# First two weight pieces of an input projection in one pass over x, loaded by the scalar engine's queue

## Chip, cores and metric

One core of a Trainium2 chip. The metric is the device time of one execution in microseconds, median over runs.

## What is computed

One layer of an encoder: neighbourhood attention beside a gated short convolution, a cross attention to a memory, and an expert-choice mixture of 16 SwiGLU experts, each followed by a layer norm. The change is in the very first product, `x @ w_in`. Cut to what matters:

```python
D_MODEL, SEQ = 1024, 512           # x: (1, 512, 1024) float32, w_in: (1024, 3072)
def hybrid_mixer(x, w_in, rpb, conv_w, w_out):
    proj = x @ w_in
    q, k, v, b_gate, c_gate, h = jnp.split(proj, [512, 1024, 1536, 2048, 2560], axis=-1)
    y_na = neighbourhood_attention(heads(q), heads(k), heads(v), rpb)
    y_conv = b_gate * short_conv(c_gate * h, conv_w)
    return jnp.concatenate([y_na, y_conv], axis=-1) @ w_out
x = layer_norm(DN_ALPHA * x + hybrid_mixer(...), ...)
x = layer_norm(DN_ALPHA * x + memory_cross_attention(...), ...)
x = layer_norm(DN_ALPHA * x + expert_choice_moe(...), ...)
```

## The kernel before

The dense weights lie in HBM as chunks of 128 partitions x 4096 floats. Chunks 0 to 7 are worked off in pieces of 1024 columns, 32 pieces in all. A piece is 8 blocks (`KT`) of 128x128: for each of the 8 blocks of x's 1024 channels, the weights of 128 output channels. Piece 0 to 3 are chunk 0, the query weights. x comes turned: block k is `x_raw[:, k, :]`, 128 channels x 512 tokens.

The products are made in parts. ScalarE rounds the weights and x to a shorter float (`hi`: `first_hi`/`hi_split` for weights, `x_hi` for x). What is left over is subtracted out: on GpSimd for the weights (`lo`, `first_lo`/`lo_split`), on VectorE for x (`x_lo`). A piece then takes 24 products of TensorE, 128x128 by 128x512, summed in one bank: 8 of hi with x_hi (L829), 8 of hi with x_lo (L831), 8 of lo with x_hi (L834). There is room for two pieces in parts (`piece[:, p % 2]`), so piece p's rounding waits until piece p - 2 has been used (`piece_used`). Banks `pj[0]` and `pj[1]` take turns in the same way (`proj_kept`), and ScalarE copies each finished bank out.

The order of the work is written out by hand, one list for each engine:

- The sync engine (SP) issues x's first transfer (blocks 0 and 1), piece 0, x's other three transfers, pieces 1 to 3, then chunk 1 and chunk 2 whole, the memory, constants and the bias (L436 to L447), and from there on waits for pieces before it loads the next chunk. All these go by one queue.
- ScalarE, L618 to L625: x block 0, half of piece 0 (4 blocks), x blocks 1 to 3, the other half of piece 0, x blocks 4 to 7, piece 1, and the tokens at the grid's edge (`edge_x`). Then for each piece its rounding and the copy of an older bank.
- GpSimd, L526 to L541: the low parts of piece 0 in two halves, then piece by piece.
- VectorE: `kv` is set to ones, then `x_lo` of the 8 blocks (L1393), then the edge's (L1396).
- TensorE: two filler products of ones whose result is not used (L887), then piece 0 in the order in which x's blocks come (`first_from_x`, L873 to L882), then pieces 1 to 7 (`from_x`), the value pieces, and so on.

Much later the 403 MB of expert weights flow through the same sync queue into an eight-slot ring; each of their loads waits for a count of TensorE's progress (`projected`, `scored`, `exp_used`).

Of the kernel before, what the change touches and what calls it, by code (L numbers as in the profile page):

```python
# [6 lines left out]
F32 = mybir.dt.float32  # L7
# [5 lines left out]
P = 128  # L13
# [90 lines left out]
PIECES = 32  # L104
# [20 lines left out]

START_FILLERS = 2


def build(nc, x, x_turned, mem_turned, dense, na_bias, conv_w, ln1_g, ln1_b,
          ln2_g, ln2_b, router, experts, ln3_g, ln3_b, consts, out):  # L130
    with ExitStack() as ctx:
# [3 lines left out]
        def sem(name):  # L135
            return ctx.enter_context(nc.semaphore(name))
# [128 lines left out]
        x_in = [sem(f"x_in{m}") for m in range(KT // 2)]  # L265
        first_in = sem("first_in")
        first_hi, first_lo, ones_set = sem("first_hi"), sem("first_lo"), sem("ones_set")
        res_in = sem("res_in")
        q_in = [sem(f"q_in{m}") for m in range(1, 4)]
        mem_in, cst_in, small_in = (sem(n) for n in ("mem_in", "cst_in", "small_in"))  # L270
# [48 lines left out]
        def pre_flat(c):  # L319
            return ring[:, PRE_SLOT[c] * SLOT:(PRE_SLOT[c] + 1) * SLOT]  # L320
# [12 lines left out]
        def raw_piece(p):  # L333
            flat = pre_flat(PIECE_CHUNK[p])[:, 1024 * (p % 4):1024 * (p % 4) + 1024]
            return flat.rearrange("p (k n) -> p k n", k=KT)

        def piece_used(eng, p):
# [67 lines left out]
        def _(sp):  # L405
# [19 lines left out]
            def load_x(m):  # L425
                k = slice(2 * m, 2 * m + 2)
                sp.dma_start(x_raw[:, k, :], x_turned[:, k, :]).then_inc(x_in[m], 16)

            def load_first():
                sp.dma_start(raw_piece(0), dense[0, :, 0:1024].rearrange("p (k n) -> p k n", k=KT)).then_inc(first_in, 16)  # L430

            def load_q(m):
                sp.dma_start(raw_piece(m), dense[0, :, 1024 * m:1024 * m + 1024].rearrange("p (k n) -> p k n", k=KT))\
                    .then_inc(q_in[m - 1], 16)

            load_x(0)  # L436
            load_first()
            for m in range(1, KT // 2):
                load_x(m)
            for m in range(1, 4):  # L440
                load_q(m)
# [5 lines left out]
            sp.dma_start(bias_room[1], na_bias[:, 4096:6144]).then_inc(bias_in, 16)  # L447
            sp.wait_ge(lo_split, 3)
            load_pre(CH_MK)
            sp.wait_ge(lo_split, 7)  # L450
            load_pre(CH_MV)
            sp.wait_ge(lo_split, 11)
            load_pre(5)
            for c, done in ((6, 15), (7, 19), (CH_OUT, 23), (CH_OUT + 1, 27)):
                sp.wait_ge(lo_split, done)
                load_pre(c)
# [67 lines left out]
        def _(pool):  # L524
            nc.gpsimd.memset(neg_half, -0.5).then_inc(half_set, 1)
            for a in range(2):  # L526
                k = slice(4 * a, 4 * a + 4)
                pool.wait_ge(first_hi, a + 1)
                nc.gpsimd.tensor_tensor(piece[:, 0, 1, k, :], raw_piece(0)[:, k, :], piece[:, 0, 0, k, :].bitcast(F32),
                                        ALU.subtract).then_inc(first_lo, 1)  # L530
# [7 lines left out]

            for p in range(1, PIECES):
                pool.wait_ge(hi_split, p)  # L540
                nc.gpsimd.tensor_tensor(piece[:, p % 2, 1, :, :], raw_piece(p), piece[:, p % 2, 0, :, :].bitcast(F32),  # L541
                                        ALU.subtract).then_inc(lo_split, 1)
                if p in POOL_EARLY:
                    out_low(POOL_EARLY[p])
# [34 lines left out]
        def _(act):  # L579
# [10 lines left out]
            def split(p):  # L590
                if p < 4:
                    act.wait_ge(q_in[p - 1], 16)
                else:
                    chunk_in(act, PIECE_CHUNK[p])
                if p >= 2:
                    piece_used(act, p - 2)
                nc.scalar.activation(piece[:, p % 2, 0, :, :], raw_piece(p), ACT.Copy).then_inc(hi_split, 1)  # L597
# [13 lines left out]

            def split_first(a):
                k = slice(4 * a, 4 * a + 4)
                act.wait_ge(first_in, 16)
                nc.scalar.activation(piece[:, 0, 0, k, :], raw_piece(0)[:, k, :], ACT.Copy).then_inc(first_hi, 1)

            split_x(0)
            split_first(0)  # L618
            for k in range(1, 4):
                split_x(k)  # L620
            split_first(1)
            for k in range(4, KT):
                split_x(k)
            split(1)
            nc.scalar.activation(edge_x[0].rearrange("p k (s t) -> p k s t", s=2), edge_tokens(x_raw), ACT.Copy)                .then_inc(edge_hi_kept, 1)  # L625
# [30 lines left out]
            for u in range(NU):  # L656
# [10 lines left out]
                if u == NU - 1:  # L667
                    act.wait_ge(lo_split, PIECES - 1)
                    chunk_in(act, CH_OUT + 1)
                    split_out(4)  # L670
                    act.wait_ge(pv_done, u - 1)
                    keep_turn(TN_NA + u, prT[u % 2])
# [15 lines left out]
                if u == 7:  # L688
                    chunk_in(act, CH_OUT)
                    split_out(0)  # L690
                elif u == 12:
                    act.wait_ge(lo_split, PIECES - 3)
                    split_out(1)
                elif u == 14:
                    act.wait_ge(projected, PIECE_PJ[PIECES - 2] + 1)
                    split_out(2)
# [115 lines left out]
        def _(pe):  # L812
# [8 lines left out]
            def from_x(p):  # L821

                n = PIECE_PJ[p]
                hi, lo = piece[:, p % 2, 0], piece[:, p % 2, 1]
                if n >= 2:
                    pe.wait_ge(proj_kept[n % 2], n // 2)
                pe.wait_ge(hi_split, p)
                for k in range(KT):
                    nc.tensor.matmul(pj[n % 2][:, :], hi[:, k, :], x_hi[:, k, :], start=k == 0, stop=False)  # L829
                for k in range(KT):  # L830
                    nc.tensor.matmul(pj[n % 2][:, :], hi[:, k, :], x_lo[:, k, :], start=False, stop=False)  # L831
                pe.wait_ge(lo_split, p)
                for k in range(KT):
                    mm = nc.tensor.matmul(pj[n % 2][:, :], lo[:, k, :], x_hi[:, k, :], start=False, stop=k == KT - 1)  # L834
                mm.then_inc(projected, 1)
# [10 lines left out]
            def v_from_x(p):  # L846
# [4 lines left out]
                if k0 == 0:  # L851
                    pe.wait_ge(edge_hi_kept, 1)
                    pe.wait_ge(edge_lo_kept, 1)
                pe.wait_ge(hi_split, p)
                for j in range(2):
                    for a in range(4):
                        nc.tensor.matmul(px[a][:, :], key_x(0, k0 + j, a), hi[:, j, :], start=k0 + j == 0, stop=False)
                        nc.tensor.matmul(px[a][:, :], key_x(1, k0 + j, a), hi[:, j, :], start=False, stop=False)
                pe.wait_ge(lo_split, p)
                for j in range(2):  # L860
# [5 lines left out]
            def first_from_x():  # L866

                hi, lo = piece[:, 0, 0], piece[:, 0, 1]
                for k in range(KT):
                    if k % 4 == 0:  # L870
                        pe.wait_ge(first_hi, k // 4 + 1)
                    pe.wait_ge(x_hi_kept, k + 1)
                    nc.tensor.matmul(pj[0][:, :], hi[:, k, :], x_hi[:, k, :], start=k == 0, stop=False)  # L873
                    if k:
                        pe.wait_ge(x_lo_kept, k)
                        nc.tensor.matmul(pj[0][:, :], hi[:, k - 1, :], x_lo[:, k - 1, :], start=False, stop=False)
                pe.wait_ge(x_lo_kept, KT)
                nc.tensor.matmul(pj[0][:, :], hi[:, KT - 1, :], x_lo[:, KT - 1, :], start=False, stop=False)
                for k in range(KT):
                    if k % 4 == 0:  # L880
                        pe.wait_ge(first_lo, k // 4 + 1)
                    mm = nc.tensor.matmul(pj[0][:, :], lo[:, k, :], x_hi[:, k, :], start=False, stop=k == KT - 1)  # L882
                mm.then_inc(projected, 1)
# [4 lines left out]
            first_from_x()  # L888
            for p in range(1, 8):
                from_x(p)  # L890
# [9 lines left out]
            def mem_k(p):  # L900
# [3 lines left out]
                pe.wait_ge(mem_lo_split, 2)  # L904
                pe.wait_ge(hi_split, p)
# [4 lines left out]
                pe.wait_ge(lo_split, p)  # L910
                for k in range(KT):
# [3 lines left out]
            def mem_v(p):  # L915
# [8 lines left out]
                pe.wait_ge(hi_split, p)  # L924
# [5 lines left out]
                pe.wait_ge(lo_split, p)  # L930
                last = p == MV_PIECES[-1]
# [924 lines left out]
```

## Time and profile before

| what | value |
|---|---|
| median of 3 runs | 1253.47 us (1252.36 to 1255.1) |
| profiled execution | known by its span, 1250.1 us from the first to the last instruction; no own time is listed for it |
| median less that span | 3.4 us |
| TensorE busy | 1167.7 us, 93% of the span |
| DMA | 444.65 MB, mean 356 GB/s |

A busy TensorE isn't one that sets the time: its rows overlap its waits, and the DMA engines are nearly full from about 310 us to the end. The chain of work that ended last tells which of the two held the end at each moment. Times in the views are microseconds from the first instruction. SPq and ACTq are the queues of DMA issues of the sync and the scalar engine; in the DMA views they are q1 and q10. The share in a DMA queue's row is that of 16 engines' time in the stretch.

### The profile page before, as it was taken

What the parts mean: (1) busy time and instruction counts of PE and PEld (TensorE: products, weight loads), DVE (VectorE), ACT (ScalarE), POOL (GpSimd) and SP (SyncE); (2) the same over time, 40 slices, a digit from 0 to 9 for tenths busy, and PEclk for the clock granted to TensorE, in tenths of its full rate; (3) what the DMA queues carried; (4) which work ended last, traced back from release to release, by engine and by line L of the source; (5) the groups of instructions that cost most, each with busy time, mean ns of one, the idle gap of its engine ahead of it and who ended that gap; (6) DMA issues with size and microseconds to landing.
All of it is one profiled execution on the core that took longest, in us unless ns stands there. A gap on an engine that the chain in (4) does not pass through costs nothing.

```text
span 1250.1 us, 13617 instructions
## 1 busy us (share of the span) xinstructions
PE 1167.7 (93%) x5780; PEld 588.4 (47%) x5780; DVE 258.4 (21%) x485; ACT 194.3 (16%) x355; POOL 137.9 (11%) x69
## 2 busy tenths in 40 slices
PE   8999999999999999998899889988997998899996
PEld 6887778888733433432243324323432432243332
DVE  3032557627600010010001000200110020002013
ACT  4244444142000000010000001000000000000021
POOL 4454334331002000000000000000000000000001
PEclk9999999999999999999999999999999999999999
DMA  9432222247799999999999999999999999999996
GB/s 374 177 135 80 92 96 105 115 186 329 299 380 428 431 412 430 426 435 434 431 427 434 433 431 430 434 432 428 434 431 432 429 434 432 430 427 428 427 428 254
DMA packets 28068, 444.65 MB, mean 356 GB/s; under 512 B 4480, under 2 KB 4864, under 8 KB 9728
## 3 DMA queue, kind: packets, MB, share of 16 engines
q1 hardware_dynamic: 25728, 441.89, 83.9%
q10 hardware_dynamic: 2304, 2.24, 0.5%
q8 instruction: 27, 0.44, 0.1%
q14 instruction: 9, 0.07, 0.0%
HBM read 442.02 MB, written 2.10 MB: 355 GB/s over the span
## 4 chain that ended last, share of the span: by engine, by line
PE 65%; DMA 30%; DVE 2%; ACT 1%; issue 1%; POOL 0%; SPq 0%; DVEq 0%; POOLq 0%; ACTq 0%
DMA ring<-in_w_exp 30%; PE bank L1317 17%; PE bank L1365 14%; PE bank L1188 5%; PE bank L1279 4%; PE bank L829 3%; PE bank L831 3%; PE bank L834 3%; PE bank L1013 1%; PE bank L1015 1%; PE bank L1014 1%; PE bank L1247 1%; PE bank L818 1%; PE bank L1349 1%; PE bank L969 1%
## 5 line engine op out<-in xcount | busy, mean ns | idle before, releaser
L1317 PE MATMUL bank<-ring,yt 128*64 128x512 f32 x2000 | 450.3, 604 | 43.5 <-DMA ring<-in_w_exp 43.4
L1317 PEld LDWEIGHTS bank<-ring,yt 128*64 128x64 f32 x2000 | 145.4, 139 | 337.1 <-issue 287.7
L1365 PE MATMUL bank<-ring,yt 128*64 128x512 f32 x944 | 214.2, 607 | 21.5 <-DMA ring<-in_w_exp 16.6
L1365 PEld LDWEIGHTS bank<-ring,yt 128*64 128x64 f32 x944 | 68.0, 139 | 146.8 <-issue 130.3
L1717 DVE TENSOR_TENSOR work<-bank,work 128x512 f32<-128x512 f32 x32 | 22.1, 692 | 378.0 <-PE bank L1317 378.0
L767 ACT ACTIVATE work<-bank 128x512 f32<-128x512 f32 x32 | 19.1, 597 | 484.5 <-PE bank L1317 484.5
L552 POOL TENSOR_SCALAR stat<-stat 128x1 f32<-128x1 f32 x4 | 2.5, 618 | 832.5 <-ACT work L808 832.4
L541 POOL TENSOR_TENSOR piece<-ring,piece 128x1024 fp32r<-128x1024 f32 x31 | 74.3, 2397 | 91.2 <-ACT piece L597 91.2
L1728 DVE TENSOR_TENSOR xT<-bank,xT 128x512 f32<-128x512 f32 x56 | 38.7, 692 | 137.1 <-PE bank L1279 137.1
L1188 PE MATMUL bank<-yt,res 128*128 128x128 f32 x512 | 60.0, 276 | 0.0
L1188 PEld LDWEIGHTS bank<-yt,res 128*128 128x128 f32 x512 | 58.4, 192 | 0.8 <-issue 0.8
L1279 PE MATMUL bank<-yt 128*128 128x512 f32 x112 | 54.5, 619 | 0.0
L771 ACT ACTIVATE yt<-bank 128x512 f32<-128x512 f32 x31 | 18.5, 597 | 198.5 <-PE bank L1349 194.5
L597 ACT ACTIVATE piece<-ring 128x1024 fp32r<-128x1024 f32 x31 | 32.8, 1059 | 89.8 <-PE bank L834 56.8
L829 PE MATMUL bank<-x_hi,piece 128*128 128x512 f32 x152 | 39.3, 401 | 0.0
L831 PE MATMUL bank<-x_lo,piece 128*128 128x512 f32 x152 | 37.6, 390 | 0.0
L834 PE MATMUL bank<-x_hi,piece 128*128 128x512 f32 x152 | 37.6, 390 | 0.0
L784 ACT ACTIVATE yt<-bank 64x512 f32<-64x512 f32 x28 | 16.5, 591 | 129.8 <-PE bank L1365 129.4
L1279 PEld LDWEIGHTS bank<-yt 128*128 128x128 f32 x112 | 17.8, 188 | 36.4 <-DVE xT L1728 18.4
L1679 DVE COPY yt<-bank 128x512 f32<-128x512 f32 x16 | 11.1, 692 | 106.9 <-PE bank L1188 106.9
L1709 DVE COPY yt<-bank 128x512 f32<-128x512 f32 x7 | 4.8, 692 | 131.2 <-PE bank L1295 131.2
L829 PEld LDWEIGHTS bank<-x_hi,piece 128*128 128x128 f32 x152 | 27.6, 188 | 8.2 <-issue 2.0
(246 smaller groups left out, 1072.7 us busy)
## 6 DMA issues: line engine op xcount, KB each, us to landing
ring<-in_w_exp SPq DMA_DIRECT2D x66, 4096.0 KB, 29.9
ring<-in_w_exp SPq DMA_DIRECT2D x39, 2048.0 KB, 29.1
ring<-in_dense SPq DMA_DIRECT2D x12, 2048.0 KB, 7.8
ring<-in_w_exp SPq DMA_DIRECT2D x6, 3072.0 KB, 28.3
ring<-in_w_exp SPq DMA_DIRECT2D x14, 1024.0 KB, 28.0
ring<-in_x_turned SPq DMA_DIRECT2D x4, 512.0 KB, 6.6
ring<-in_dense SPq DMA_DIRECT2D x4, 512.0 KB, 9.2
res<-in_na_bias SPq DMA_DIRECT2D x1, 2048.0 KB, 27.1
```

The costliest lines, as they stand in the source:

```text
L541: nc.gpsimd.tensor_tensor(piece[:, p % 2, 1, :, :], raw_piece(p), piece[:, p % 2, 0, :, :].bitcast(F32), ALU.subtract).then_inc(lo_split, 1)
L597: nc.scalar.activation(piece[:, p % 2, 0, :, :], raw_piece(p), ACT.Copy).then_inc(hi_split, 1)
L767: nc.scalar.activation(silu[g], bank[2 * g][:, :], ACT.Silu).then_inc(silu_done, 1)
L829: nc.tensor.matmul(pj[n % 2][:, :], hi[:, k, :], x_hi[:, k, :], start=k == 0, stop=False)
L831: nc.tensor.matmul(pj[n % 2][:, :], hi[:, k, :], x_lo[:, k, :], start=False, stop=False)
L834: mm = nc.tensor.matmul(pj[n % 2][:, :], lo[:, k, :], x_hi[:, k, :], start=False, stop=k == KT - 1)
L1188: mm = nc.tensor.matmul(pv[k // 4][:, P * (k % 4):P * (k % 4) + P], res[:, t, P * k:P * k + P], pick[:, t].rearrange("p e n -> p (e n)"), ...
L1279: mm = nc.tensor.matmul(pv[(c + 1) % 2][:, :], scat[:, t, :], ye[:, 512 * n:512 * n + 512], start=True, stop=True)
L1317: mm = nc.tensor.matmul(bank[2 * g + n % 2][64 * c:64 * c + 64, :], xeT[:, kk, 64 * e:64 * e + 64], exp_rhs(j, first, k, c), start=kk == 0 ...
L1365: mm = nc.tensor.matmul(bank[5][64 * n:64 * n + 64, :], hidT[:, s, 64 * c:64 * c + 64], exp_rhs(j, first, s, n), start=(g, c, s) == (0, 0, ...
L1717: nc.vector.tensor_tensor(hid[g], bank[2 * g + 1][:, :], silu[g], ALU.mult).then_inc(hid_ready, 1)
L1728: nc.vector.tensor_tensor(y, pv[(c + 1) % 2][:, :], y, ALU.add).then_inc(mix_kept, 1)
```

## The change

Pieces 0 and 1 are taken together in one pass over x's blocks. They are loaded as four transfers (`FIRST_LOADS`), each with two blocks of both pieces, by ScalarE's queue ahead of its first rounding. In HBM each partition's part of such a transfer is two runs of 256 floats. The sync queue no longer loads pieces 0 and 1. ScalarE rounds a transfer's 128 x 512 elements between the two x blocks of the same number, GpSimd makes low parts by transfer. TensorE does both pieces' products block by block; the low products of piece 0 are mixed in, those of piece 1 follow at the end. There are three start fillers for two, and a half-wide one inside each of the first three blocks. The counts of `hi_split` and `lo_split` now start at piece 2, which `nth(p)` takes care of wherever they are waited for.

```diff
-START_FILLERS = 2
+START_FILLERS = 3
+FIRST_PIECES = 2
+FIRST_LOADS = KT // 2
...
-        first_in = sem("first_in")
+        first_in = [sem(f"first_in{g}") for g in range(FIRST_LOADS)]
...
+        def nth(p):
+            return p - FIRST_PIECES + 1
+
+        def first_raw(g):
+            flat = pre_flat(0)[:, 0:1024 * FIRST_PIECES]
+            return flat.rearrange("p (a k n) -> p a k n", a=FIRST_PIECES, k=KT)[:, :, 2 * g:2 * g + 2, :]
+
+        def first_part(g, part):
+            return piece[:, :, part, 2 * g:2 * g + 2, :]
...
-            load_x(0)
-            load_first()
-            for m in range(1, KT // 2):
+            for m in range(KT // 2):
                 load_x(m)
-            for m in range(1, 4):
+            for m in range(FIRST_PIECES, 4):
                 load_q(m)
...
-            for a in range(2):
-                k = slice(4 * a, 4 * a + 4)
-                pool.wait_ge(first_hi, a + 1)
-                nc.gpsimd.tensor_tensor(piece[:, 0, 1, k, :], raw_piece(0)[:, k, :], piece[:, 0, 0, k, :].bitcast(F32),
+            for g in range(FIRST_LOADS):
+                pool.wait_ge(first_hi, g + 1)
+                nc.gpsimd.tensor_tensor(first_part(g, 1), first_raw(g), first_part(g, 0).bitcast(F32),
                                         ALU.subtract).then_inc(first_lo, 1)
...
-            def split_first(a):
-                k = slice(4 * a, 4 * a + 4)
-                act.wait_ge(first_in, 16)
-                nc.scalar.activation(piece[:, 0, 0, k, :], raw_piece(0)[:, k, :], ACT.Copy).then_inc(first_hi, 1)
-
-            split_x(0)
-            split_first(0)
-            for k in range(1, 4):
-                split_x(k)
-            split_first(1)
-            for k in range(4, KT):
-                split_x(k)
-            split(1)
+            def load_first(g):
+                src = dense[0, :, 0:1024 * FIRST_PIECES].rearrange("p (a k n) -> p a k n", a=FIRST_PIECES, k=KT)
+                act.dma_start(first_raw(g), src[:, :, 2 * g:2 * g + 2, :]).then_inc(first_in[g], 16)
+
+            def split_first(g):
+                act.wait_ge(first_in[g], 16)
+                nc.scalar.activation(first_part(g, 0), first_raw(g), ACT.Copy).then_inc(first_hi, 1)
+
+            for g in range(FIRST_LOADS):
+                load_first(g)
+            for g in range(FIRST_LOADS):
+                split_x(2 * g)
+                split_first(g)
+                split_x(2 * g + 1)
...
             def first_from_x():
 
-                hi, lo = piece[:, 0, 0], piece[:, 0, 1]
+                def product(n, k, w, of, stop=False):
+                    return nc.tensor.matmul(pj[n][:, :], piece[:, n, w, k, :], of[:, k, :],
+                                            start=k == 0 and w == 0 and of is x_hi, stop=stop)
+
                 for k in range(KT):
-                    if k % 4 == 0:
-                        pe.wait_ge(first_hi, k // 4 + 1)
+                    if k % 2 == 0:
+                        pe.wait_ge(first_hi, k // 2 + 1)
                     pe.wait_ge(x_hi_kept, k + 1)
-                    nc.tensor.matmul(pj[0][:, :], hi[:, k, :], x_hi[:, k, :], start=k == 0, stop=False)
+                    for n in range(FIRST_PIECES):
+                        product(n, k, 0, x_hi)
+                    if k < 3:
+                        nc.tensor.matmul(px[0][:, 0:256], kv[:, 0:P], kv[:, 0:256], start=True, stop=True)
                     if k:
                         pe.wait_ge(x_lo_kept, k)
-                        nc.tensor.matmul(pj[0][:, :], hi[:, k - 1, :], x_lo[:, k - 1, :], start=False, stop=False)
+                        for n in range(FIRST_PIECES):
+                            product(n, k - 1, 0, x_lo)
+                    if k % 2 and k > 1:
+                        pe.wait_ge(first_lo, k // 2)
+                        for m in (k - 3, k - 2):
+                            product(0, m, 1, x_hi)
                 pe.wait_ge(x_lo_kept, KT)
-                nc.tensor.matmul(pj[0][:, :], hi[:, KT - 1, :], x_lo[:, KT - 1, :], start=False, stop=False)
-                for k in range(KT):
-                    if k % 4 == 0:
-                        pe.wait_ge(first_lo, k // 4 + 1)
-                    mm = nc.tensor.matmul(pj[0][:, :], lo[:, k, :], x_hi[:, k, :], start=False, stop=k == KT - 1)
+                product(0, KT - 1, 0, x_lo)
+                pe.wait_ge(first_lo, FIRST_LOADS)
+                for m in (KT - 2, KT - 1):
+                    mm = product(0, m, 1, x_hi, stop=m == KT - 1)
+                mm.then_inc(projected, 1)
+                product(1, KT - 1, 0, x_lo)
+                for m in range(KT):
+                    mm = product(1, m, 1, x_hi, stop=m == KT - 1)
                 mm.then_inc(projected, 1)
...
-            for p in range(1, 8):
+            for p in range(FIRST_PIECES, 8):
                 from_x(p)
```

ScalarE at the start of the program, before (line numbers of the kernel before; `ring` holds the raw weights and x):

```order
L610 ACT_TABLE_LOAD
L610 ACTIVATE x_hi<-ring 128x512 [waits x_in0]
L615 ACTIVATE piece<-ring 128x512 [waits first_in]
L610 ACTIVATE x_hi<-ring 128x512 [waits x_in0]
L610 ACTIVATE x_hi<-ring 128x512 [waits x_in1] x2
L615 ACTIVATE piece<-ring 128x512 [waits first_in]
L610 ACTIVATE x_hi<-ring 128x512 [waits x_in2] x2
L610 ACTIVATE x_hi<-ring 128x512 [waits x_in3] x2
L597 ACTIVATE piece<-ring 128x1024 [waits q_in1]
```

And with the change (line numbers of the changed kernel):

```order
L619 DMA ring<-in_dense 128x2x256 x4
L615 ACT_TABLE_LOAD
L615 ACTIVATE x_hi<-ring 128x512 [waits x_in0]
L623 ACTIVATE piece<-ring 128x2x256 [waits first_in0]
L615 ACTIVATE x_hi<-ring 128x512 [waits x_in0]
...
L615 ACTIVATE x_hi<-ring 128x512 [waits x_in3]
L623 ACTIVATE piece<-ring 128x2x256 [waits first_in3]
L615 ACTIVATE x_hi<-ring 128x512 [waits x_in3]
L631 ACTIVATE edge_x_70<-ring 128x1024
L602 ACTIVATE piece<-ring 128x1024 [waits projected,q_in2]
```

Four DMA issues stand ahead of the table load, and the rounding of x's last block now follows a wait for the fourth weight transfer.

TensorE at x's blocks 6 and 7, before:

```order
L873 MATMUL bank<-x_hi,piece 128x512 [waits x_hi_kept]
L876 MATMUL bank<-x_lo,piece 128x512 [waits x_lo_kept]
L878 MATMUL bank<-x_lo,piece 128x512 [waits x_lo_kept]
L882 MATMUL bank<-x_hi,piece 128x512 [waits first_lo]
L882 MATMUL bank<-x_hi,piece 128x512 x3
L829 MATMUL bank<-x_hi,piece 128x512 [waits hi_split]
```

And with the change, from block 6 to the first product of piece 2:

```order
L875 MATMUL bank<-x_hi,piece 128x512 [waits x_hi_kept,first_hi]
L875 MATMUL bank<-x_hi,piece 128x512
L875 MATMUL bank<-x_lo,piece 128x512 [waits x_lo_kept]
...
L875 MATMUL bank<-x_hi,piece 128x512 [waits x_hi_kept]
...
L875 MATMUL bank<-x_hi,piece 128x512 [waits first_lo]
...
L875 MATMUL bank<-x_lo,piece 128x512
L875 MATMUL bank<-x_hi,piece 128x512 x8
L835 MATMUL bank<-x_hi,piece 128x512 [waits hi_split,proj_kept0]
```

Block 6's products now wait for a weight transfer of their own (`first_hi`), where only x was waited for; the next piece is piece 2 and waits for bank 0's copy too.

## Rows read from the trace of the kernel before

**Rows 1.** The page: span, and the chain's shares by line

```profile
span 1250.1 us, 13617 instructions
...
DMA ring<-in_w_exp 30%; PE bank L1317 17%; PE bank L1365 14%; PE bank L1188 5%; PE bank L1279 4%; PE bank L829 3%; PE bank L831 3%; PE bank L834 3%; PE bank L1013 1%; PE bank L1015 1%; PE bank L1014 1%; PE bank L1247 1%; PE bank L818 1%; PE bank L1349 1%; PE bank L969 1%
```

**Rows 2.** Chain of waits, 0 to 22 us: start us, us, what

```profile
1.65 6.16 DMA ring<-in_x_turned
...
10.06 3.45 DVE x_lo L1393 x4
...
19.52 1.81 PE bank L834 x8
```

**Rows 3.** Chain of waits, whole span: the first long wait for a DMA

```profile
489.72 22.18 DMA ring<-in_w_exp
```

**Rows 4.** Three issuing lines: duration ns, first and last start us; time to landing

```profile
L427 SPq DMA_DIRECT2D ring<-in_x_turned x4: 384/428/840, 0.7 to 2.6; - x4
...
DMA to landing us min/median/max: 4.0/6.6/7.8
...
L433 SPq DMA_DIRECT2D ring<-in_dense x3: 446/447/466, 3.5 to 4.5; - x3
...
DMA to landing us min/median/max: 8.8/9.6/10.4
...
L407 SPq DMA_DIRECT2D ring<-in_dense x2: 440/470/500, 5.0 to 5.5; - x2
...
DMA to landing us min/median/max: 14.8/16.9/19.1
```

**Rows 5.** DMA queues, 0 to 60 us: packets, MB, share of 16 engines

```profile
q1 hardware_dynamic: 2304, 17.02, 72.0%
q10 hardware_dynamic: 1728, 0.15, 2.6%
```

**Rows 6.** DMA queues, 40 to 41 us

```profile
DMA packets 79, 0.05 MB, mean 55 GB/s; under 512 B 43, under 2 KB 78, under 8 KB 78
...
q10 hardware_dynamic: 78, 0.04, 19.9%
```

**Rows 7.** DMA queues at 275 to 276 us, then at 36 to 37 us

```profile
q1 hardware_dynamic: 22, 0.36, 87.3%
q10 hardware_dynamic: 20, 0.08, 20.5%
...
q1 hardware_dynamic: 26, 0.41, 96.8%
q10 hardware_dynamic: 27, 0.00, 1.5%
```

**Rows 8.** Timeline of the start, and one stretch with clock (ninth column) by windows

```profile
1.45 3.70 PE L887 MATMUL bank<-kv 128*128 128x512 f32 x4 [1.45 <-DVE kv L1390]
...
4.78 0.63 ACT L610 ACTIVATE x_hi<-ring 128x512 fp32r<-128x512 f32 x1 [2.76 <-DMA ring<-in_x_turned]
...
6.25 0.63 ACT L615 ACTIVATE piece<-ring 128x512 fp32r<-128x512 f32 x1 [0.84 <-DMA ring<-in_dense]
...
6.93 1.02 PE L873 MATMUL bank<-x_hi,piece 128*128 128x512 f32 x2 [1.78 <-ACT piece L615]
...
10.39 0.63 PE L873 MATMUL bank<-x_hi,piece 128*128 128x512 f32 x1
...
10.82 0.63 PE L876 MATMUL bank<-x_lo,piece 128*128 128x512 f32 x1
...
12.30 1.06 ACT L597 ACTIVATE piece<-ring 128x1024 fp32r<-128x1024 f32 x1 [0.72 <-DMA ring<-in_dense]
...
8.30:11.70 3.40, 3.18 (x7) 2.13 (x7) 3.34 (x5) 3.29 (x7) 1.55 (x1) 0.51 1.02 365
```

**Rows 9.** ScalarE's DMA issues: one line's durations, and one long issue

```profile
L587 ACTq DMA_DIRECT2D cw<-in_conv_w x3: 448/521/528, 32.4 to 33.4; - x3
...
33.94 4.60 ACTq L588 DMA_DIRECT2D wr<-in_router  x1
```

More of the change, by code:

```diff
@@ L265, in build @@
         x_in = [sem(f"x_in{m}") for m in range(KT // 2)]
-        first_in = sem("first_in")
+        first_in = [sem(f"first_in{g}") for g in range(FIRST_LOADS)]
         first_hi, first_lo, ones_set = sem("first_hi"), sem("first_lo"), sem("ones_set")
         res_in = sem("res_in")
-        q_in = [sem(f"q_in{m}") for m in range(1, 4)]
+        q_in = [sem(f"q_in{m}") for m in range(FIRST_PIECES, 4)]
         mem_in, cst_in, small_in = (sem(n) for n in ("mem_in", "cst_in", "small_in"))
@@ L427, in load_x @@
                 sp.dma_start(x_raw[:, k, :], x_turned[:, k, :]).then_inc(x_in[m], 16)
-            def load_first():
-                sp.dma_start(raw_piece(0), dense[0, :, 0:1024].rearrange("p (k n) -> p k n", k=KT)).then_inc(first_in, 16)
             def load_q(m):
                 sp.dma_start(raw_piece(m), dense[0, :, 1024 * m:1024 * m + 1024].rearrange("p (k n) -> p k n", k=KT))\
-                    .then_inc(q_in[m - 1], 16)
-            load_x(0)
-            load_first()
-            for m in range(1, KT // 2):
+                    .then_inc(q_in[m - FIRST_PIECES], 16)
+            for m in range(KT // 2):
                 load_x(m)
-            for m in range(1, 4):
+            for m in range(FIRST_PIECES, 4):
                 load_q(m)
@@ L447, in _ @@
             sp.dma_start(bias_room[1], na_bias[:, 4096:6144]).then_inc(bias_in, 16)
-            sp.wait_ge(lo_split, 3)
+            sp.wait_ge(lo_split, nth(3))
             load_pre(CH_MK)
-            sp.wait_ge(lo_split, 7)
+            sp.wait_ge(lo_split, nth(7))
             load_pre(CH_MV)
-            sp.wait_ge(lo_split, 11)
+            sp.wait_ge(lo_split, nth(11))
             load_pre(5)
             for c, done in ((6, 15), (7, 19), (CH_OUT, 23), (CH_OUT + 1, 27)):
-                sp.wait_ge(lo_split, done)
+                sp.wait_ge(lo_split, nth(done))
                 load_pre(c)
@@ L537, in out_low @@
                 nc.gpsimd.tensor_tensor(lo, raw, hi.bitcast(F32), ALU.subtract).then_inc(out_lo_pool, 1)
-            for p in range(1, PIECES):
-                pool.wait_ge(hi_split, p)
+            for p in range(FIRST_PIECES, PIECES):
+                pool.wait_ge(hi_split, nth(p))
                 nc.gpsimd.tensor_tensor(piece[:, p % 2, 1, :, :], raw_piece(p), piece[:, p % 2, 0, :, :].bitcast(F32),
@@ L591, in split @@
                 if p < 4:
-                    act.wait_ge(q_in[p - 1], 16)
+                    act.wait_ge(q_in[p - FIRST_PIECES], 16)
                 else:
                     chunk_in(act, PIECE_CHUNK[p])
-                if p >= 2:
-                    piece_used(act, p - 2)
+                piece_used(act, p - 2)
                 nc.scalar.activation(piece[:, p % 2, 0, :, :], raw_piece(p), ACT.Copy).then_inc(hi_split, 1)
@@ L667, in _ @@
                 if u == NU - 1:
-                    act.wait_ge(lo_split, PIECES - 1)
+                    act.wait_ge(lo_split, nth(PIECES - 1))
                     chunk_in(act, CH_OUT + 1)
@@ L691, in _ @@
                 elif u == 12:
-                    act.wait_ge(lo_split, PIECES - 3)
+                    act.wait_ge(lo_split, nth(PIECES - 3))
                     split_out(1)
@@ L826, in from_x @@
                     pe.wait_ge(proj_kept[n % 2], n // 2)
-                pe.wait_ge(hi_split, p)
+                pe.wait_ge(hi_split, nth(p))
                 for k in range(KT):
@@ L831, in from_x @@
                     nc.tensor.matmul(pj[n % 2][:, :], hi[:, k, :], x_lo[:, k, :], start=False, stop=False)
-                pe.wait_ge(lo_split, p)
+                pe.wait_ge(lo_split, nth(p))
                 for k in range(KT):
@@ L853, in v_from_x @@
                     pe.wait_ge(edge_lo_kept, 1)
-                pe.wait_ge(hi_split, p)
+                pe.wait_ge(hi_split, nth(p))
                 for j in range(2):
@@ L858, in v_from_x @@
                         nc.tensor.matmul(px[a][:, :], key_x(1, k0 + j, a), hi[:, j, :], start=False, stop=False)
-                pe.wait_ge(lo_split, p)
+                pe.wait_ge(lo_split, nth(p))
                 for j in range(2):
@@ L904, in mem_k @@
                 pe.wait_ge(mem_lo_split, 2)
-                pe.wait_ge(hi_split, p)
+                pe.wait_ge(hi_split, nth(p))
                 for k in range(KT):
@@ L909, in mem_k @@
                     nc.tensor.matmul(acc, hi[:, k, :], m_lo[:, k, :], start=False, stop=False)
-                pe.wait_ge(lo_split, p)
+                pe.wait_ge(lo_split, nth(p))
                 for k in range(KT):
@@ L923, in mem_v @@
                         pe.wait_ge(proj_kept[(PJ_MV + t) % 2], (PJ_MV + t) // 2)
-                pe.wait_ge(hi_split, p)
+                pe.wait_ge(hi_split, nth(p))
                 for j in range(2):
@@ L929, in mem_v @@
                                              start=k0 + j == 0 and m is m_hi, stop=False)
-                pe.wait_ge(lo_split, p)
+                pe.wait_ge(lo_split, nth(p))
                 last = p == MV_PIECES[-1]
```

## The prediction

> **What bounds the kernel now.** I read the page first: its chain of waits is TensorE's own lines and, for 30%, transfers of expert weights [rows 1]. In order of time the two parts are apart: from 14 us on the chain is TensorE work and the short steps between its stages, and the first long wait for expert weights comes at 489.72 us [rows 3]. The loads of expert weights are started by TensorE's progress (the waits on projected, scored and exp_used), so a microsecond gained or lost before 14 us moves all behind it by a microsecond, as far as these rows tell. I count it in full.
>
> The chain of the first 22 us [rows 2] tells what sets the start: x's second transfer lands at 7.81, then come ScalarE's roundings of x, then four of VectorE's subtractions (10.06 to 13.51), then the low products of piece 0 and piece 1's 24 products, the last eight from 19.52 to 21.33. From there TensorE goes on without a gap. So 21.33 us, the end of piece 1, is the mark that the change has to beat.
>
> **What the transfers give.** Now x's four transfers, pieces 0, 1, 2, 3 and chunk 1, 2 stand in one queue. x's first is issued at 0.73 and lands 4.0 us later, at 4.8; piece 3, issued at 4.5, lands after 10.4, at 14.9 [rows 4]. In between lie seven transfers of 4 KB rows. Packets are the contiguous runs: in the first 60 us the sync queue moved 2304, which is 16 transfers x 128 rows plus 16 small ones for each transfer, and the scalar queue 1728, which is three conv_w loads of 512 four-byte runs, 128 router rows, and 4 x 16 small ones [rows 5]. Hence on each of 16 DMA engines a load of 128 rows is 8 packets and a small one. The price of a 4 KB packet is (14.9 - 4.8) / 56 = 0.18 us. Chunk 2 (16 KB rows, 16 packets behind piece 3) lands at 5.5 + 19.1 = 24.6: (24.6 - 14.9) / 16 = 0.61 us each. A line through both gives 0.07 us for 1 KB. Its lower bound is a quarter of a 4 KB packet, 0.045, its upper bound a whole one, 0.18. The nearest row: at 40 to 41 us the scalar queue, almost alone, moved 78 packets in 19.9% of 16 engine-microseconds, 43 of them under 512 B, so 35 of about 1 KB at no more than 3.2 / 35 = 0.09 [rows 6]. I take 0.07.
>
> **The change part by part.**
> *Transfers.* Pieces 0 and 1 come as four transfers of 128 x 2 runs of 1 KB: 17 packets on each engine per transfer, 68 in all. They leave on the scalar queue, beside the sync queue's 9 per transfer (x four times, pieces 2 and 3, chunks 1 and 2). What decides is how an engine shares itself between two queues. The trace has it twice: at 275 us both queues are full, the sync queue with 16 KB and the scalar queue with 4 KB packets, and they move 22 against 20; at 36 us it is 26 packets of 16 KB against 27 of 4 bytes [rows 7]. One packet of one, one packet of the other, whatever their size. By this the queue with the many small packets is served last.
>
> Under that alternation a landing is 3.3 us (4.8 less 8 x 0.18) plus everything moved until then. Transfer 0 ends at packet 17: 3.3 + 16 x 0.18 + 16 x 0.07 = 7.3. Transfer 1 at packet 34: 3.3 + 31 x 0.18 + 32 x 0.07 = 11.1. x's fourth at 36: about 11.4. Transfer 2 at 51, of which the other queue has spent 45 on x and pieces 2 and 3: 3.3 + 45 x 0.18 + 48 x 0.07 = 14.8. The sync queue's small loads end at packet 54, so the last 14 packets of transfer 3 each go after one of chunk 1's or 2's, 13 of these with data: 3.3 + 48 x 0.18 + 13 x 0.61 + 64 x 0.07 = 24.4 us. Before, all of pieces 0 and 1 was there at 12.3 [rows 8].
>
> By the Trainium skill ("DMA: Bandwidth & Descriptors", Queues, rings and completion order) an engine drains a whole packet of some 9 to 17 descriptors from one ring before it goes to the next; if a packet there were one transfer's share, the two queues would change over per transfer. The counts of the rows above speak against that reading; it is the first rival below.
>
> *TensorE.* Its order asks for first_hi 4 before the two products of block 6. Of 48 products 26 stand ahead of that (12 with x_hi, 10 with x_lo, 4 low ones), which are through by about 17 us; 22 are left. ScalarE needs 0.63 for the rounding, and TensorE's first product of piece 0 came 0.7 us after its landing (6.25 to 6.93) [rows 8]; so TensorE resumes at 25.1. 22 products at 1.81 / 8 = 0.227 us are 5.0 us. Before them it has been idle some 8 us. The trace shows what that costs: idle from 5.15 to 6.93, it then had a granted clock of 0.51 from 8.3 to 11.7, the 1.2 GHz level, with products 0.43 us apart (10.39, 10.82). Over 3.4 us that is 8 products where 15 were possible, 1.6 us lost. I put in the same once: bounds are 0 and all 22 products, 4.4. End of piece 1: 25.1 + 5.0 + 1.6 = 31.7, against 21.33: +10.4 us.
>
> *ScalarE.* Four DMA issues of about 0.5 us [rows 9] stand before the table load, 2.1 us. It had been idle for 2.76 us before x's first block [rows 8], which now comes later. Cost 0. A long issue like the 4.60 us one, with 1,584 packets queued ahead [rows 9], would add 4.1, 1.3 beyond that idle time, and be hidden as well: until transfer 0 lands at 7.3 one rounding waits. In the new order each block pair's rounding stands behind a wait for its transfer, so x_hi 7, the edge rounding and VectorE's work on both are queued behind transfer 3; all of these are 0.5 to 1 us and end before their products are due (x_hi 7 at 25.6).
> *Fillers.* Two start fillers are four rows in 3.70 us [rows 8], so the third ends at 7.0, and the three small ones inside the pass are half as wide, 0.9 each at most. Products of piece 0 can't start before 8.0 and then wait for every transfer, so they cost 0; if transfers were prompt, they would cost up to 2.8.
> *GpSimd* makes the same low parts in four steps; the last one's first product is due after 11 others, 2.5 to 4.7 us behind the rounding. 0.
> *Sync queue.* Two issues fewer. Chunks 1 and 2 land up to 4.5 us later (64 x 0.07), at 24 and 29; their first users are pieces 4 and 8, whose turns come ten later as well. 0.
>
> **Sum:** +10.4 us on a span of 1250.1, so 1260.5. The runs shown have their median 3.4 us above the span: **1263.9 us**. Case alone: -1.6 for the clock and -1.8 for packets by bytes, +3 for a longer slow clock or dearer packets: 1260.5 to 1267.
>
> **The rivals.**
> *Queues change over per transfer* (the page's reading): transfer 3 lands right behind x's fourth, 3.3 + 32 x 0.18 + 64 x 0.07 = 13.5; resume at 14.2, 22 products, 19.2: 2.1 us ahead, less up to 1.6 if the clock falls as now. 1251.4 to 1253.0, no change that can be told. For it: the rows counted were not at the program's start, when both queues are empty. Against: the same counts with three mixes of size. 0.17.
> *Faster:* the same, and 1 KB packets go by bytes, 0.045: landing at 3.3 + 5.8 + 2.9 = 12.0, and with a full clock, which the fillers hold, TensorE ends at 12.7 + 5.0 = 17.7, 3.6 ahead: 1249.9. The point from which it decides: transfer 3 must land before 13. Against it the 0.09 bound of [rows 6], and 48 products from 7 us on need 10.9 us by themselves. 0.10.
> *Slower still:* a 1 KB packet takes a 4 KB packet's time between two queues, 64 x 0.11 = +7: 1271. 0.05.
> *The transfers aren't split as written* (a row's two runs as one packet of 2 KB): 36 packets in place of 68 would end with x's fourth, the first rival's time; the 1728 packets counted for runs of 4 bytes leave it little; it is within that 0.17.
>
> **How the numbers follow.** Alternation 0.68, slower still 0.05, per transfer 0.17, faster 0.10. A measurement can tell about 0.2%, 2.5 us. Faster 0.10, same 0.17, slower 0.73. The forecast is the likeliest case's 1263.9, its own range 1260.5 to 1267; the range that leaves out no more than 2 in 10 has to take in the per-transfer case: 1251 to 1267.
>
> **What would show it.** In the changed trace: both queues with near equal packet counts from 3 to 15 us; the four dense transfers landing at about 7, 11, 15 and 24 us; TensorE idle from about 17 to 25 for ScalarE's rounding, and ScalarE for a DMA into ring; a granted clock of 0.5 behind it; the first product of piece 2 at 31 to 32. If the fourth lands by 14, the alternation is wrong at the start of a program and so is the forecast; if it lands at 24 and the time rises by less than 7, the loss does not carry to the end.

## The result and the profile after

The changed kernel takes 1260.38 us (median of 4 runs, 1259.24 to 1262.87), the kernel before 1253.36 us beside it. The ratio is 1.0060, 95% interval 1.0048 to 1.0072: slower by 6.0 to 9.0 us. The forecast was 1263.9 us, range 1251 to 1267; the time also lies just under the likeliest case's own range, 1260.5 to 1267.

The chain of waits of the changed kernel, 0 to 40 us (start us, us, what), answers to [rows 2]:

```profile
2.29 18.97 DMA ring<-in_dense
...
21.27 0.64 ACT piece L623
...
21.96 7.89 PE bank L875 x22
29.84 1.81 PE bank L835 x8
```

The chain's first DMA wait is no longer for x but for the fourth weight transfer, issued at 2.29 and landed at 21.25 us. Piece 1 ends at 29.84 us, where it ended at 21.33: 8.5 us later. Its landings by issuing line, which answer to [rows 4]:

```profile
L619 ACTq DMA_DIRECT2D ring<-in_dense x4: 482/486/1073, 0.7 to 2.3; - x4
...
DMA to landing us min/median/max: 5.1/10.0/19.0
```

The DMA queues of the changed kernel at 4, 7, 9, 14 and 16 us, one microsecond each (packets, MB, share of 16 engines; q1 the sync queue, q10 ScalarE's):

```profile
q10 hardware_dynamic: 143, 0.15, 49.1%
q1 hardware_dynamic: 41, 0.10, 36.7%
...
q1 hardware_dynamic: 82, 0.33, 80.5%
q10 hardware_dynamic: 82, 0.08, 23.6%
...
q1 hardware_dynamic: 83, 0.32, 79.6%
q10 hardware_dynamic: 83, 0.08, 22.8%
...
q1 hardware_dynamic: 27, 0.44, 104.2%
q10 hardware_dynamic: 28, 0.03, 8.2%
...
q1 hardware_dynamic: 27, 0.44, 104.5%
q10 hardware_dynamic: 26, 0.03, 7.7%
```

From 7 to 18 us the counts are nearly equal in each microsecond (58 against 53 where they differ most), whatever the sizes: 82 against 82 and 83 against 83 with x's 4 KB packets, 27 against 28 and 27 against 26 with the 16 KB packets of chunks 1 and 2. Before 7 us they are not: at 4 to 5 us ScalarE's queue moved 143 packets and the sync queue 41, and when the first weight transfer was through, at 5.9 us, 272 against 210. What shares the engines out there is not shown. From 14 us on the weights that TensorE waits for get 0.03 MB in a microsecond, and chunks 1 and 2, whose first user is piece 4 with its first product at 40.7 us, get 0.44.

What ScalarE and TensorE do meanwhile, in the timeline (start us, us, engine, line, op; behind it the idle time before and what ended it):

```profile
9.99 0.63 ACT L623 ACTIVATE piece<-ring 128x512 fp32r<-128x512 f32 x1 [1.93 <-DMA ring<-in_dense]
...
13.15 0.63 ACT L623 ACTIVATE piece<-ring 128x512 fp32r<-128x512 f32 x1 [1.49 <-DMA ring<-in_dense]
...
15.78 0.61 PE L875 MATMUL bank<-x_hi,piece 128*128 128x512 f32 x2
21.27 0.63 ACT L623 ACTIVATE piece<-ring 128x512 fp32r<-128x512 f32 x1 [6.45 <-DMA ring<-in_dense]
...
21.96 1.22 PE L875 MATMUL bank<-x_hi,piece 128*128 128x512 f32 x2 [5.56 <-ACT piece L623]
```

And by windows (busy us and count of PE, PEld, DVE, ACT, POOL, then the granted clock, the DMA share, GB/s):

```profile
16.00:21.90 5.90, 0.40 (x2) 0.00 (x0) 0.30 (x1) 0.63 (x2) 0.00 (x0) 0.90 1.04 438
21.90:27.30 5.40, 5.34 (x13) 4.18 (x14) 2.49 (x2) 1.47 (x3) 1.28 (x1) 0.50 1.02 425
```

TensorE is idle for 5.6 us, and behind that its granted clock is 0.50, the 1.2 GHz level, for 5.4 us: 12 or 13 products where 24 would fit. The shift is carried along: a row of the chain that stood at 455.42 us before stands at 464.04, 8.6 later (before, then with the change).

```profile
455.42 17.32 PE bank L1317 x80
...
464.04 17.32 PE bank L1337 x80
```

### The profile page after: what moved, and what is told of

The parts are those of the page before. It is cut to its first block, busy times and chain, and to the rows that moved or that the text cites. A ratio compares the mean times of both kernels' runs of the same rounds, so it can differ in the third digit from the quotient of the medians.

```text
span 1261.0 us, 13639 instructions
## 1 busy us (share of the span) xinstructions
PE 1172.9 (93%) x5788; PEld 591.7 (47%) x5788; DVE 258.0 (20%) x485; ACT 194.7 (15%) x356; POOL 137.8 (11%) x70
## 4 chain that ended last, share of the span: by engine, by line
PE 64%; DMA 31%; DVE 2%; ACT 1%; issue 1%; POOL 0%; ACTq 0%; DVEq 0%; SPq 0%; POOLq 0%
DMA ring<-in_w_exp 30%; PE bank L1337 17%; PE bank L1385 14%; PE bank L1208 5%; PE bank L1299 4%; PE bank L835 3%; PE bank L837 3%; PE bank L840 3%; DMA ring<-in_dense 2%; PE bank L1033 1%; PE bank L1035 1%; PE bank L1034 1%; PE bank L1267 1%; PE bank L824 1%; PE bank L1369 1%; PE bank L989 1%
## 5 line engine op out<-in xcount | busy, mean ns | idle before, releaser
L835 PE MATMUL bank<-x_hi,piece 128*128 128x512 f32 x144 | 37.3, 401 | 0.0
L840 PE MATMUL bank<-x_hi,piece 128*128 128x512 f32 x144 | 35.6, 389 | 0.0
L1699 DVE COPY yt<-bank 128x512 f32<-128x512 f32 x16 | 11.1, 692 | 106.9 <-PE bank L1208 106.9
```

## The experiments

All are edits of the changed kernel. The last column is the median and the ratio to the kernel before with its interval; "end of piece 1" is the chain's row of the first product of piece 2.

| kernel | fourth transfer landed | end of piece 1 | chain's mark near 455 us | median us, ratio |
|---|---|---|---|---|
| before | (12.3, piece 1) | 21.33 | 455.42 | 1253.36 |
| changed | 21.25 | 29.84 | 464.04 | 1260.38, 1.0060 (1.0048 to 1.0072) |
| e1 one queue | 12.8 | 19.72 | 453.87 | 1251.16, 0.9987 (0.9978 to 0.9996) |
| e2 sync queue holds back | 11.9 | 20.92 | 455.21 | 1252.09, 0.9998 (0.9989 to 1.0007) |
| e3 runs of 2 KB | 12.8 | 19.99 | 454.16 | 1251.74, 0.9990 (0.9981 to 0.9999) |
| e4 the same, old fillers | 12.3 | 19.93 | 454.08 | 1251.10, 0.9987 (0.9978 to 0.9996) |
| e5 runs of 512 B | 35.5 (third 32.50) | 43.56 | 477.68 | 1275.30, 1.0181 (1.0166 to 1.0197) |
| e6 2 KB in one queue | 12.9 | 19.44 | 455.18 | 1251.06, 0.9987 (0.9978 to 0.9996) |
| e7 chunks held back | 14.6 | 21.42 | 457.10 | 1253.53, 1.0005 (0.9996 to 1.0014) |
| e8 fillers in the idle stretch | 20.9 | 26.85 | 461.07 | 1260.05, 1.0063 (1.0047 to 1.0078) |
| e9 changed once more | 21.5 | 29.68 | 463.84 | 1260.64, 1.0061 (1.0047 to 1.0074) |
| e10 as e8, once more | 21.31 | 27.30 | 461.55 | 1258.56, 1.0045 (1.0032 to 1.0059) |

(e1 to e4 ran beside 1253.50 us of before, e5 to e8 beside 1252.57, e9 and e10 beside 1253.55.)

**e1, one queue.**

```diff
+            def load_first(g):
+                src = dense[0, :, 0:1024 * FIRST_PIECES].rearrange("p (a k n) -> p a k n", a=FIRST_PIECES, k=KT)
+                sp.dma_start(first_raw(g), src[:, :, 2 * g:2 * g + 2, :]).then_inc(first_in[g], 16)
+
             for m in range(KT // 2):
                 load_x(m)
+                load_first(m)
...
-            for g in range(FIRST_LOADS):
-                load_first(g)
```

> The changed kernel with its four weight transfers (still 1 KB runs) issued by the sync engine, each behind the x transfer of its number, nothing on the scalar queue at the start. Theory (an engine alternates packet by packet between two queues, so the queue with many small packets ends behind chunks 1 and 2): in one queue the fourth weight transfer lands when x and itself are through, 12 to 15 us instead of 21.3, and piece 1 ends at 18.8 to 20.6: 0.7 to 2.5 us ahead of the kernel before, so 1250.9 to 1252.7. Rival (runs of 1 KB are slow by themselves, whatever the queue): the fourth lands near 21 and the time stays near 1260.

Its chain, 0 to 32 us:

```profile
2.15 6.58 DMA ring<-in_dense
...
8.75 0.64 ACT piece L628
...
10.60 9.11 PE bank L878 x40
19.72 1.84 PE bank L838 x8
```

The same 1 KB runs, the same order on TensorE: piece 1 ends at 19.72, 1.6 us ahead of the kernel before and 10.1 ahead of the changed one. Behind the small filler of block 2 the chain is 40 products without a wait, so from there TensorE is the bound of the pass. Small runs are not slow by themselves, and the pass and its fillers aren't what cost the time. The time is 0.9987 of before, inside what was expected.

**e2, the sync queue holds back.**

```diff
+            sp.wait_ge(first_in[FIRST_LOADS - 1], 16)
             for m in range(FIRST_PIECES, 4):
                 load_q(m)
```

> The changed kernel, weights still on the scalar queue in 1 KB runs, but the sync engine waits for the fourth of them before it issues piece 2 and all that follows. Alternation theory: only x's 36 packets compete with the 68, the rest go alone; the fourth lands at 12.5 to 13.5, piece 1 ends at about 19, time about 1251, though piece 2 and 3 then land at 16 to 18. Rival (small runs slow): no nearer than 18 us and 1257 or more. Rival (scalar queue served late whatever the other holds): unchanged, 1260.

At 8 to 9 us, with x in the sync queue, and at 10 to 11 us, with nothing more in it:

```profile
q1 hardware_dynamic: 93, 0.32, 79.5%
q10 hardware_dynamic: 93, 0.09, 25.1%
...
q10 hardware_dynamic: 368, 0.36, 108.3%
q1 hardware_dynamic: 5, 0.00, 0.3%
```

ScalarE's queue is untouched, and all that changed is what stands in the other one. As soon as that is empty the weights' rate goes from 93 packets in a microsecond to 368. The fourth transfer landed at 11.9, ahead of the 12.5 to 13.5 expected, but piece 1 ended at 20.92 and not at about 19, since the second transfer is held up by x as it was (9.95 us) and block 2 starts at 10.65. Time as before, 0.9998, 1 us over what was expected.

**e3, runs of 2 KB.** The first 2048 columns of chunk 0 are laid out by transfer, in HBM and on chip:

```diff
+    first = out[0, :, 0:1024 * FIRST_PIECES].reshape(P, FIRST_PIECES, FIRST_LOADS, 2, P)
+    out[0, :, 0:1024 * FIRST_PIECES] = first.transpose(0, 2, 1, 3, 4).reshape(P, -1)
...
-                act.dma_start(first_raw(g), src[:, :, 2 * g:2 * g + 2, :]).then_inc(first_in[g], 16)
+                act.dma_start(pre_flat(0)[:, 512 * g:512 * g + 512], dense[0, :, 512 * g:512 * g + 512])\
+                    .then_inc(first_in[g], 16)
```

> The changed kernel with the first two pieces laid out in HBM and on chip so that each partition's part of a transfer is one run of 2 KB: 9 packets per engine and transfer as x has, same bytes, same two queues. Alternation theory: the fourth weight transfer lands with x's fourth, at 11 to 12.5; TensorE's own work from 6.6 on (48 products and three small fillers, some 12.3 us) then sets the end of piece 1 at about 18.9: 2.4 ahead of before, 1251. If the order of TensorE or the fillers were what costs time, it would stay near 1260.

At 9 to 10 us:

```profile
q1 hardware_dynamic: 78, 0.27, 67.2%
q10 hardware_dynamic: 78, 0.13, 34.6%
```

Two queues again, equal counts again, but now the weights get twice the bytes for each turn, and x a little less. The fourth lands at 12.8, 0.4 behind x's fourth (11 to 12.5 was expected). Piece 1 ends at 19.99, 9.85 us ahead of the changed kernel but 1.1 later than expected, 1251.74 us.

**e4, the old fillers with e3's transfers.**

```diff
-START_FILLERS = 3
+START_FILLERS = 2
...
-                    if k < 3:
-                        nc.tensor.matmul(px[0][:, 0:256], kv[:, 0:P], kv[:, 0:256], start=True, stop=True)
```

> As the 2 KB runs, with two start fillers and none inside the pass, as before the change. If the fillers only cost TensorE time once transfers are prompt, piece 1 ends 1.3 us earlier than with them (about 17.6, 1249.7). If without them the granted clock falls to half for 3.4 us as in the kernel before, it ends 1.6 us later less the 1.3: about the same as with them, 1251 to 1251.5.

TensorE in e4's timeline:

```profile
8.91 1.05 PE L875 MATMUL bank<-x_lo,piece 128*128 128x512 f32 x2
9.77 1.05 PE L875 MATMUL bank<-x_hi,piece 128*128 128x512 f32 x2
...
11.13 0.62 PE L875 MATMUL bank<-x_hi,piece 128*128 128x512 f32 x2
```

From 7.0 to 10.6 us the products are 0.43 us apart (two from 8.91 to 9.77), though the granted clock reads 1.00 there; from 11.1 on 0.23. In e3 the first pair, ahead of any small filler, takes 0.57 us, as a pair behind a wait does later on (9.73 to 10.30); in the changed kernel the first pair takes 0.77, and from the second on all is at full speed. So the third start filler does its work, and the four fillers cost about what the slow products would: 19.93 against 19.99, and no difference in time. That was the second of the two cases expected.

**e5, twice the packets.** Each transfer in two, of one block of both pieces:

```diff
+                for k in range(2):
+                    act.dma_start(first_raw(g)[:, :, k:k + 1, :], src[:, :, 2 * g + k:2 * g + k + 1, :])\
+                        .then_inc(first_in[g], 16)
```

> The changed kernel with each weight transfer cut into two of 512 B runs: the same bytes on the same queue in twice the packets, 136 on each engine instead of 68. Alternation theory: the sync queue has given 54 packets when x and pieces 2 and 3 are through (13 to 14 us); then the scalar queue's other 82 each wait for one of chunks 1 and 2 and of the loads behind them (54 packets, to about 36 us), so the fourth pair lands at 30 to 36 and the time is 1270 to 1277. Rival (a packet costs a fixed time of its own, at most 0.1 us): 64 packets more are at most 6 us more, the fourth at 25 to 27 and the time near 1266 at most.

The DMA queues at 20 to 21 us, and the chain:

```profile
q1 hardware_dynamic: 27, 0.44, 104.2%
q10 hardware_dynamic: 26, 0.01, 4.3%
```

```profile
3.75 28.75 DMA ring<-in_dense
...
33.21 10.36 PE bank L877 x32
43.56 1.84 PE bank L837 x8
```

The weights' bytes fall to 0.01 MB in a microsecond. The chain's row ends with the third pair, at 32.50 us, where the third transfer landed at 13.1 in the changed kernel; TensorE's 32 products stand behind it. The last pair landed at 35.5, 14.3 later than the fourth transfer of the changed kernel, for 64 packets with data more on each engine: 0.22 us each, more than any packet of 512 B takes by itself (e2 moved 1 KB packets at 16 / 368 = 0.043 us). The time, 1275.3 us, is what the alternation gave; the rival's bound was 1266.

**e7, only chunks 1 and 2 held back.**

```diff
+            sp.wait_ge(first_in[FIRST_LOADS - 1], 16)
             load_pre(1)
```

> The changed kernel with chunks 1 and 2 alone held back until the fourth weight transfer has landed; pieces 2 and 3 still go beside it. Alternation theory: the loss comes from the 16 KB packets, so the fourth lands at 14.5 to 15 instead of 21.3, TensorE is idle for under 1 us, piece 1 ends at 20 to 21, time 1252 to 1253.5. If pieces 2 and 3 were the load that pushed it back, it would stay above 1257.

```profile
1.77 11.35 DMA ring<-in_dense
...
13.83 7.59 PE bank L876 x32
21.42 1.84 PE bank L836 x8
```

The chain now passes through the third transfer (issued 1.77, landed 13.12); the fourth is no longer in it. Piece 1 ends 8.4 us earlier than in the changed kernel and 0.1 later than before; the time is that of before. So the 8.5 us lie in the 16 KB packets of chunks 1 and 2. Pieces 2 and 3 beside the weights cost 0.5 (e2, without them, ended at 20.92). That it ended at 21.42 and not by 21, as expected, comes with the third transfer, which landed at 13.12, no earlier than in the changed kernel.

**e8, e9 and e10, the clock.** Six filler products where TensorE is idle:

```diff
                 for k in range(KT):
+                    if k == 6:
+                        for _ in range(6):
+                            nc.tensor.matmul(px[0][:, :], kv[:, 0:P], kv[:, 0:512], start=True, stop=True)
```

> The changed kernel with six full-width filler products put before block 6, in TensorE's idle time (16 to 21.9 us); the transfers are untouched. After the fourth transfer the 22 products took 7.9 us, where 22 x 0.227 are 5.0. Theory (the half clock behind the idle stretch costs the 2.9): the granted clock stays 1.0, piece 1 ends at 27 instead of 29.8 and the time is 1257 to 1258. Rival (the products wait for VectorE and GpSimd anyway): 29 or more and 1260.

In e8 the products behind the fourth transfer (chain, then the window in which the changed kernel had a clock of 0.50; L881 is the six fillers, two rows each):

```profile
16.47 5.15 PE bank L881 x12
21.62 5.23 PE bank L875 x22
26.85 1.84 PE bank L835 x8
```

```profile
21.90:27.30 5.40, 5.40 (x25) 4.45 (x24) 2.50 (x2) 2.98 (x5) 2.24 (x2) 1.00 1.01 419
```

With the clock kept, the 22 products take 5.2 us, not 7.9. But the time came out at 1260.05 us, ratio 1.0063 (1.0047 to 1.0078), where 1257 to 1258 was expected. Since e8 and the changed kernel had been compared across chips and with four runs each, both went again, on one chip.

> The changed kernel once more, beside the next one on the same chip, since the earlier comparison of the two was across chips and with four runs each. Start shift 8.6 us; if it carries in full the ratio is 1.0069, near 1261 to 1262 against 1253.

> The changed kernel with six filler products in the idle stretch, once more, same chip as the changed kernel. Its profile had piece 1 done 3.0 us earlier and the shift unchanged at 461 us, but its time was no lower. Theory (all behind the start carries, the earlier runs differ by the spread of the expert stream): 2.5 to 3.5 us under the changed kernel, ratio to before 1.0045. Rival (the expert stream gives back what is gained): within 1 us of the changed kernel.

The chains of e9 and of e10 behind the fourth transfer:

```profile
22.21 7.47 PE bank L875 x22
```

```profile
22.02 5.29 PE bank L875 x22
```

The changed kernel took 1260.64 us (ratio 1.0061, 1.0047 to 1.0074), about 1 us under what was expected, the one with fillers 1258.56 (1.0045, 1.0032 to 1.0059): 2.1 us less, between the 2.5 to 3.5 of the theory and the rival's 1. In these two profiles the mark near 455 us stands at 463.84 and 461.55, 2.3 apart. On this chip what the clock cost carried to the end: each of the five runs with fillers was faster than each of the five without, 1259.51 us at most against 1259.75 at least. e8 is the same kernel as e10 and showed nothing of it, with its shift at the mark as small (461.07). What lies behind the mark (span less mark) took 796.8 us in e8's profile and 794.6 in e10's, so what e8's time lacks was lost there. The gain at piece 1 and at the mark is shown twice, that in the time once, and what the expert stream lost in e8 stays open.

**e6, what the runs pointed to.** e3's layout, all eight transfers in the sync queue in turn, and no small filler inside block 2 (`k < 2` for `k < 3`).

> What the runs so far point to: 2 KB runs, all in the sync queue with each weight transfer behind the x transfer of its number, and no small filler after block 2 (it stood in the chain with 0.43 us). The second weight transfer should land at about 8.3 instead of 8.7 and TensorE go through from there without a wait: piece 1 ends at 18.8 to 19.0, 2.4 ahead of the kernel before, 1250 to 1251. If the chain's start doesn't carry to the end, it stays at 1251.2 as the best of the earlier ones.

Piece 1 ends at 19.44, the earliest of all, but 0.5 us later than expected. TensorE starts its first product at 6.96; 48 x 0.227 and two small fillers of 0.43 from there would end at 18.7, and the first pair was slow, 0.88 us. So little is left to gain. The time, 1251.06 us, is that of e1 and e4. Four kernels beat both the one before and the changed one: e1, e4 and e6 by 0.13% of before (interval 0.04 to 0.22%), e3 by 0.10%. The intervals exclude no change, but only just, and the gain is under the 0.2% of the forecast's bound.

## Why the prediction was right

The forecast case happened: packet by packet, the two queues alternated, though only from about 7 us on and not from 3 as forecast, the fourth transfer landed behind the first part of chunks 1 and 2, and TensorE waited for it. e2, e3, e5 and e7 each change one side of that (what the other queue holds, the size of a turn, the number of turns, the large packets alone) and move the landing as it says. The Trainium skill ("DMA: Bandwidth & Descriptors", "Queues, rings and completion order") says that an engine drains 9 to 17 descriptors of one ring before it changes over. No trace here agrees with it for descriptors as the profile counts packets. The first rival had the queues change over with each transfer's share, which would have given 1251.4 to 1253.0 us: by turns of 17 and 9 packets the counts would be near two to one, and they are 82 to 82 and 28 to 27.

The size came out less well than the mechanism. The time missed the case's own range by 0.1 us, and the wider range reached down to 1251 for a case that did not happen. The start moved by 8.5 us for 10.4, the time by 7.0.

- *Landings.* 7.3, 11.1, 14.8 and 24.4 us were forecast; 5.9, 10.0, 13.1 and 21.3 were measured. The mis-sized term is, for the most part, "64 x 0.07" for the 1 KB packets. Beside 4 KB packets a pair took 16 / 83 = 0.193 us, so the small one added 0.013 to the 0.18 of the large one, and beside 16 KB packets a pair took 16 / 27 = 0.59, no more than the 0.61 of one alone. By itself a 1 KB packet takes 0.043 (e2), a quarter of a 4 KB packet, so the straight line through 4 and 16 KB was too high even for one queue, and beside another the value lay under both bounds. With 0.013 for 0.07 the sum gives 20.7 for the last landing. The first transfer was early also because the sync queue had moved 13 packets on each engine by then and not 17. The other term, 13 packets of 16 KB, held: 204 of them on 16 engines, 8.1 us from the third landing to the fourth, where 13 x 0.61 is 7.9.
- *TensorE behind it.* Resumed 0.7 us after the landing, 22 products left, as forecast. "1.6 us" for the clock was too little: 7.9 us less 5.2 in e8 is 2.7, and e9 against e10 gives 2.2. I had taken the length of the one slow stretch before, 3.4 us; this one lasted 5.4. That stretch was also a poor example: the start fillers' rows and the products from 6.93 to 8.3 us stood at half speed too, ahead of the first record of 0.51, so it was not simply the price of the idle time from 5.15 to 6.93. The bound that I had written, 4.4, held.
- *Sum.* The two errors, 3.1 us too late and 1.1 too little, go against each other and leave 31.7 forecast against 29.84: 10.4 against 8.5 us. That the sum came this near is in part luck.
- *Carry.* Counted in full. Up to the mark near 455 us it is so to 0.2 us in the changed kernel, in e1 to e5 and in e8 to e10. The medians then show +7.0 for +8.5, +7.1 for +8.4 (e9), +5.0 for +6.0 (e10), +7.5 for +5.5 (e8) and +22.7 for +22.2 (e5), so up to 2 us get lost or gained behind the mark. Two profiles of one kernel differ there as much: span less mark is 797.0 us in the changed kernel's first profile and 795.0 in e9's (before 794.7), so this is no cost of the change that the traces show; what does it was not tried. e6 and e7 lose some 1.6 us ahead of the mark, nearly all of it at one place, a second fall of the clock: in the three chains below (before, e7, e6) the same 12 products take 1.53, 2.81 and 2.45 us, and the granted clock read 0.50 at 334 to 336 us in e7 and at 332 to 334 in e6, where it stayed 1.00 in the kernel before. Each is one execution, so what brought it on is not shown.

```profile
333.30 1.53 PE bank L840 x12
...
333.45 2.81 PE bank L847 x12
...
331.52 2.45 PE bank L849 x12
```

- *Costs put at nothing.* ScalarE's DMA issues took 2.62 us and the table load followed, and x's first block was waited for all the same. GpSimd, VectorE, fillers and the sync queue stand nowhere in the chain.

## What to carry to other kernels

When a transfer on the path is moved to a second DMA queue, count packets and not bytes: here, from 7 us on and with both queues full, it got one packet for each of the other's, so 1 KB runs beside 16 KB rows were served 0.03 of 0.47 MB in a microsecond. Three ways out worked here: the same queue in the order of need (e1), longer runs (e3), or a neighbour that waits (e2, e7). And a stall of TensorE can cost more than its length: behind 5.6 us idle came 5.4 us at half the clock, behind 1.4 us idle at 9.3 to 10.7 the clock stayed 1.00. Fillers in the long stall bought that part back at the end of piece 1, and in one of two comparisons in the time.

## What was not expected of the hardware

A 1 KB packet costs almost nothing beside a 4 KB packet of the other queue (0.193 us for the pair, 0.18 for one 4 KB packet in one queue), and the 1 KB runs alone moved at 0.36 MB in a microsecond, like 4 KB rows in the kernel before (16 x 4 KB in 0.18 us is 0.364): on this chip and at this size small runs were not slow, only few turns were.

The granted clock in the records is 1.00 at the start of the program, yet in e4 products at 7.0 to 10.6 us stand 0.43 us apart, and the start fillers' rows 0.86 us, where in e8 the same rows inside the program take 5.15 / 12 = 0.43. So in these traces the granted clock of the first microseconds did not agree with the spacing of equal rows, and the spacing is what told the speed.
